# Eight groups of a conditioning product, moved from TensorE to POOL

## The reference, cut to what matters

```python
mod = silu(c) @ w_ada + b_ada          # w_ada 1024 x 6144: six vectors of 1024
h   = rmsnorm(x) * (1 + scale) + shift # the first two, for the token mixer
...                                    # mixer: window attention, gated scan, grouped attention
x   = x + gate_1 * mixer(h)            # the third
h2  = rmsnorm(x) * (1 + scale_2) + shift_2   # the fourth and fifth
x   = x + gate_2 * moe(h2)             # the sixth
```

## Time and profile before

| | |
|---|---|
| median of 3 executions | 820.46 us |
| span of the profiled execution | 816.3 us |
| PE busy | 758.7 us, 93% |
| POOL busy | 25.0 us, 3% |
| DVE busy / ACT busy | 274.9 us / 104.2 us |
| mean granted TensorE clock | 0.990 |

### The profile page before, as it was taken

One profiled execution on the slowest core, in us unless ns is written; L12 is line 12 of the kernel. 1 busy time (PEld: TensorE's weight loads), 2 busy tenths in 40 slices (PEclk: granted clock), 3 DMA queues, 4 the chain that ended last, 5 costly groups with the idle time before them and its releaser, 6 DMA issues.

```text
span 816.3 us, 8564 instructions
## 1 busy us (share of the span) xinstructions
PE 758.7 (93%) x3562; PEld 437.1 (54%) x3562; DVE 274.9 (34%) x484; ACT 104.2 (13%) x185; POOL 25.0 (3%) x44
## 2 busy tenths in 40 slices
PE   5889989999999999999999999995999999999994
PEld 2344676666774377666676587443443443443431
DVE  1422325544200647433332323246203212212323
ACT  4010110000001322212212500020000000000011
POOL 0100000000000006000000000000000000000000
PEclk9999999999999999999999999998999999999998
DMA  9842243020210322754336727951899999987951
GB/s 376 335 200 104 103 136 148 0 104 1 104 52 1 119 100 102 298 206 175 141 136 271 307 106 325 395 190 42 348 373 419 429 419 420 430 338 295 427 216 54
DMA packets 13571, 178.46 MB, mean 219 GB/s; under 512 B 1504, under 2 KB 1632, under 8 KB 2528
## 3 DMA queue, kind: packets, MB, share of 16 engines
q1 hardware_dynamic: 13104, 176.56, 54.0%
q10 hardware_dynamic: 432, 1.40, 0.4%
HBM read 176.91 MB, written 1.05 MB: 218 GB/s over the span
## 4 chain that ended last, share of the span: by engine, by line
PE 86%; DVE 6%; DMA 3%; issue 3%; DVEq 1%; ACT 1%; SPq 0%; POOL 0%; PEldq 0%; ACTq 0%
PE bank L971 20%; PE bank L657 15%; PE bank L651 10%; PE bank L661 8%; PE bank L674 5%; PE bank L959 4%; PE bank L703 4%; PE bank L680 3%; DMA sb<-front_w 3%; PE bank L1015 2%; PE bank L645 2%; PE bank L802 2%; PE bank L823 2%; PE bank L667 2%; PE bank L810 1%
## 5 line engine op out<-in xcount | busy, mean ns | idle before, releaser
L971 PE MATMUL bank<-sb 128*64 128x512 f32 x768 | 166.8, 593 | 3.4 <-DVE sb L1427 2.8
L657 PE MATMUL bank<-sb 128*128 128x256 f32 x576 | 128.2, 381 | 2.4 <-PE bank L645 1.3
L657 PEld LDWEIGHTS bank<-sb 128*128 128x128 f32 x576 | 108.1, 190 | 23.2 <-issue 9.1
L971 PEld LDWEIGHTS bank<-sb 128*64 128x64 f32 x768 | 54.4, 137 | 113.7 <-issue 109.8
L651 PE MATMUL bank<-sb 128*128 128x512 f32 x192 | 85.4, 602 | 3.9 <-DVE sb L1106 3.6
L661 PE MATMUL bank<-sb 128*128 128x512 f32 x160 | 70.0, 593 | 0.3 <-PE bank L657 0.3
L1153 DVE COPY sb<-bank 128x512 f32<-128x512 f32 x45 | 29.4, 686 | 117.7 <-PE bank L810 83.2
L651 PEld LDWEIGHTS bank<-sb 128*128 128x128 f32 x192 | 36.6, 194 | 48.6 <-issue 45.4
L661 PEld LDWEIGHTS bank<-sb 128*128 128x128 f32 x160 | 29.9, 190 | 36.4 <-issue 36.4
L674 PE MATMUL bank<-sb 128*128 128x256 f32 x192 | 42.2, 380 | 0.6 <-PE bank L674 0.6
L1437 DVE TENSOR_TENSOR sb<-sb,bank 128x512 f32<-128x512 f32 x8 | 5.5, 688 | 101.7 <-PE bank L971 89.3
(11 more groups left out here) (210 smaller groups left out, 581.4 us busy)
## 6 DMA issues: line engine op xcount, KB each, us to landing
sb<-expert_w SPq DMA_DIRECT2D x48, 2048.0 KB, 12.2
sb<-front_w SPq DMA_DIRECT2D x32, 2048.0 KB, 8.1
sb<-xcT SPq DMA_DIRECT2D x2, 1024.0 KB, 7.5
sb<-na_bias SPq DMA_DIRECT2D x1, 1536.0 KB, 10.9
sb<-front_w SPq DMA_DIRECT2D x1, 1024.0 KB, 5.0
sb<-b_rows SPq DMA_DIRECT2D x1, 1024.0 KB, 10.3
sb<-x_nat SPq DMA_DIRECT2D x1, 1024.0 KB, 12.3
out<-sb SPq DMA_DIRECT2D x4, 256.0 KB, 2.6
```

The costliest lines, as they stand in the source:

```text
L657: ins = pe.matmul(ps[:, c * L:(c + 1) * L], lhs(w, k, (2 * i + c) * P), hT[:, k, 0:L], start=(k == 0), stop=(k == KD - 1))
L971: ins = pe.matmul(bank[e * CAP:(e + 1) * CAP, :], lhsT[:, k, e * CAP:(e + 1) * CAP], slot[s + e][:, k * cols[0] + cols[1]:k * cols[0] + co ...
```

## The change: groups 4 to 11 made on POOL

TensorE no longer multiplies the slots of ada4 to ada11. POOL, after its work on the grouped attention's q and k, multiplies the whole slot (128x4096) by silu(c), one value per partition and block of 512, in place; three adds fold 4096 columns to 2048, 1024 and 512, the last one into `ada_place(g)`. A semaphore `w_summed` then releases the slot and the turn. `ada_turn` sums over the partitions: one matmul with `ones` for the row groups, the same four transposes for the others, of which DVE now reduces all 128 columns. The group's turn stands one step behind the last fill of the next gate: before steps 8, 10, 12 and 14 for groups 4 to 7, behind step 15 for groups 8 to 11. From the third group on, POOL waits ahead of its multiply until the turn of the group two before it is done (they share a place). The fillers are one per step.

```diff
+POOLED = [f"ada{g}" for g in range(4, 12)]
+GROUPS = ["ada0", "ada2", "ada1", "ada3", "ff"] + [n for n in FRONT[5:] if n not in POOLED]
...
+for _i, _n in enumerate(FILLER):
+    FILLER_AT[_i * STEPS // len(FILLER)].append(_n)
+ADA_TURNS = {i: [] for i in range(STEPS + 1)}
+for _g in range(4, 12):
+    _next = [n for n in FRONT[FRONT.index(f"ada{_g}"):] if n[:4] == "gate"]
+    _at = [i for i in range(STEPS) if _next and fill_no(_next[0], 1) in FILLER_AT[i]] + [STEPS]
+    ADA_TURNS[min(_at[0] + 1, STEPS)].append(_g)
...
+        def wait_free(eng, n):
+            eng.wait_ge(w_summed if FRONT[n] in POOLED else w_used, taken(n))
...
+            pool.wait_ge(c_ready, 1)
+            for i, name in enumerate(POOLED):
+                n, g = FRONT.index(name), int(name[3:])
+                pool.wait_ge(w_in_[SLOT_OF[n]], 16 * (len(earlier(n)) + 1))
+                if i > 1:
+                    pool.wait_ge(shared_ready, shared_no("ada", g - 2) + 1)
+                w = slot[SLOT_OF[n]]
+                wk = w.rearrange("p (k c) -> p k c", k=KD)
+                link(pool.tensor_tensor(wk, wk, cvec[:, :, 0:1].broadcast_to([P, KD, 512]), ALU.mult))
+                link(pool.tensor_tensor(w[:, 0:2048], w[:, 0:2048], w[:, 2048:4096], ALU.add))
+                link(pool.tensor_tensor(w[:, 0:1024], w[:, 0:1024], w[:, 1024:2048], ALU.add))
+                link(pool.tensor_tensor(ada_place(g), w[:, 0:512], w[:, 512:1024], ALU.add))
+                pool.sem_inc(w_summed, 1)
...
             def ada_turn(g):
-                wait_emptied(pe, fill_no(f"ada{g}"))
+                if g < 4:
+                    wait_emptied(pe, fill_no(f"ada{g}"))
+                else:
+                    pe.wait_ge(w_summed, g - 3)
                 ps = take_shared(shared_no("ada", g))
                 src = ada_place(g)
                 if g in ROW_GROUPS:
-                    ins = pe.matmul(ps[:, :], sm("stream0"), src, start=True, stop=True)
+                    ins = pe.matmul(ps[:, :], ones, src, start=True, stop=True)
```

More of the change, by code:

```diff
@@ L51 @@
 USES = [SLOT_OF.count(s) for s in range(FSLOTS)]
-GROUPS = ["ada0", "ada2", "ada1", "ada3", "ff"] + FRONT[5:]
+POOLED = [f"ada{g}" for g in range(4, 12)]
+GROUPS = ["ada0", "ada2", "ada1", "ada3", "ff"] + [n for n in FRONT[5:] if n not in POOLED]
 def taken(n):
-    return GROUPS.index(FRONT[n]) + 1
+    return (POOLED if FRONT[n] in POOLED else GROUPS).index(FRONT[n]) + 1
 def earlier(n):
@@ L100 @@
 FILLER = [n for n in range(fill_no("gq"), fill_no("br0"))]
-def cost(n):
-    return 1 if FILLS[n][0][:3] == "ada" else 4
 FILLER_AT = {i: [] for i in range(STEPS)}
[L108 to L111, removed]
+for _i, _n in enumerate(FILLER):
[5 more added lines that the diff above has]
+    ADA_TURNS[min(_at[0] + 1, STEPS)].append(_g)
 G_STEP = [i for i in range(STEPS) if fill_no("gkv", 1) in FILLER_AT[i]][0]
@@ L122, in ada_in_step @@
 def ada_in_step(i):
-    return [int(FILLS[n][0][3:]) for n in FILLER_AT.get(i, []) if FILLS[n][0][:3] == "ada"]
+    return ADA_TURNS.get(i + 1, [])
 for _i in range(STEPS + 1):
@@ L271, in build @@
         w_in_ = [sem(f"weights_in{i}") for i in range(SLOTS)]
-        w_used = sem("weights_used")
+        w_used, w_summed = sem("weights_used"), sem("weights_summed")
         fill_ready = sem("fill_ready")
@@ L326, in _ @@
                 if earlier(n):
-                    sp.wait_ge(w_used, taken(earlier(n)[-1]))
+                    wait_free(sp, earlier(n)[-1])
                 cols = SLOT // 2 if name == "gkv" else SLOT
@@ L384, in _ @@
                 if s < FSLOTS:
-                    sp.wait_ge(w_used, taken([n for n in range(len(FRONT)) if SLOT_OF[n] == s][-1]))
+                    wait_free(sp, [n for n in range(len(FRONT)) if SLOT_OF[n] == s][-1])
                 load(s, (s % 2) * 3 + s // 2)
@@ L520, in fill @@
                         act.wait_ge(shared_ready, shared_no("ada", g - 1) + 1)
-                    elif g > 5:
-                        act.wait_ge(shared_ready, shared_no("ada", g - 2) + 1)
                     act.activation(ada_place(g), ps[:, :], ACT.Copy).then_inc(done, 1)
@@ L1085, in add_ada @@
                 else:
-                    parts = ps[:, :].rearrange("p (c q s) -> p c s q", c=4, q=4)[:, :, 0:2, :]
-                    dve.tensor_reduce(mod[:, 4 * g:4 * g + 4, :], parts, AX.X, ALU.add).then_inc(shared_out, 1)
+                    if g < 4:
+                        parts = ps[:, :].rearrange("p (c q s) -> p c s q", c=4, q=4)[:, :, 0:2, :]
+                        dst = mod[:, 4 * g:4 * g + 4, :]
+                    else:
+                        parts, dst = ps[:, :].rearrange("p (c q) -> p c q", c=4), mod[:, 4 * g:4 * g + 4, 0]
+                    dve.tensor_reduce(dst, parts, AX.X, ALU.add).then_inc(shared_out, 1)
             b_ada = sm("b_ada")
@@ L1506 @@
 SMALL = 0
-for _name, *_dims in (("ident", P), ("ones", P), ("below", P), ("stream0", P), ("iota", CAP), ("eps", 1), ("limits", MAXPASS - 1),
+for _name, *_dims in (("ident", P), ("ones", P), ("below", P), ("iota", CAP), ("eps", 1), ("limits", MAXPASS - 1),
                       ("rank", NE), ("b_ada", 48), ("g_mix", KD), ("g_ffn", KD), ("lb", 8), ("hg_g", 1),
@@ L1534, in shape_constants @@
         "below": (i[:, None] < i[None, :]).astype(f),
-        "stream0": np.tile((i[:, None] % 32 == 0).astype(f), (1, P)),
         "iota": np.tile(np.arange(CAP, dtype=f), (P, 1)),
```

## The result

The changed kernel takes 857.25 us (median of 4, 855.77 to 858.67) where the kernel before takes 820.14 (median of 4): ratio 1.0458, 95% interval 1.043 to 1.0485, 37 us slower. The forecast was 847.5 us, 27 slower. Its profiled span is 856.8 us, its mean granted clock 0.959 instead of 0.990, POOL is busy 146.9 us instead of 25.0.

A forecast was written before the change was run, and what follows sets the result against it. TensorE was taken as the bound, with 86% of the chain; fills and turns save 19.9 us, but POOL waits, gate5's load and the clock make the first branch 27.0 late: span 843.3 plus 4.2 gives 847.5 us, range 838 to 859.

The forecast's parts named there:

- the hold: Half of DVE's normalising pair stands still for a whole POOL instruction and ends 0.28 us after it.
- the walk: Step-by-step timing of the new kernel through the attention steps: first branch fill at 491.3 instead of 464.34, span 843.3 us.
- (b): Rival, chance 0.13: POOL is slower on long rows, T = 18 us a group with a multiply of 9.1; 857.6 us.
- (d): Rival, chance 0.10: stalls inside steps each cost half clock, 3 times 1.6 us, and one more hold of 4; 856 us.
- What POOL needs for a group: POOL's multiply 7.1 us and adds 4.7, 2.4 and 1.3, from slopes of shorter rows: T = 15.9 us a group.
- (c): Rival, chance 0.04: not slower, POOL at the one-input cast's pace, T = 7.5 us, pair stalls nearly vanish; 820.6 us.
- The wait at the end: Behind step 15, POOL's groups 10 and 11 take 31.8 us; turns to first branch fill 36.3 us instead of 4.5.
- the clock's 1.6: TensorE restarts at the half clock level after the long idle behind group 11: 1.6 us lost, added once.
- Waits inside the steps: DVE's normalising pairs, held beside POOL's long instructions, make steps 6, 7 and 8 late by 2.9, 5.3 and 2.1 us.
- rival (a): Chance 0.16: POOL holds DVE only briefly, stalls of steps 6 to 8 go, b_rows costs 4.5 us at step 8; 842.0 us.
- gate5's load: Load into gate4's slot, no longer covered by two ada fills: it lands at 435.7, its fill 3.4 us late.
- Nothing behind it changes: Behind the first branch fill no further cost: the expert loads keep their distance to TensorE.

## Why the prediction was right, and where it was short

The direction, the hold and the long waits came out as forecast; 847.5 was 10 us short of 857.25, and closer than the working deserves. By the walk itself the first branch fill was 11.5 us short (491.3 for 502.78) and the span 13.5 (843.3 for 856.8): 2.1 more were lost behind the branches, 4.2 us around the span instead of 1.8 gave 2.4 back, and the median lies 1.3 below the profiled execution. The number was inside the range only because this reached up to (b) and (d), and (b) did not happen, and (d) only by half. By its own steps:

- *What POOL needs for a group.* 15.5 us measured, 15.9 forecast: multiply 7.03 (7.1), adds 4.53, 2.40 and 1.28 (4.7, 2.4, 1.3). Slopes from rows of 128 to 1024 columns held up to 4096. Rivals (b) and (c) fall with it; that (b)'s 857.6 is nearly the measured time is chance.
- *The wait at the end.* From step 15's turned probabilities (465.72) to the first branch fill 37.1 us, forecast 37.9 with the clock. Four places took one of the two waits away, idle matmuls the clock's 1.6 (1.6 forecast).
- *Waits inside the steps.* Idle 1.98, 3.33 and 2.11 us in steps 6 to 8, forecast 2.9, 5.3 and 2.1. The hold itself is as forecast, the second half of a pair waits for the next instruction as well: 7.21 us for 343.64 to 350.85, the end of the first add (350.57) plus 0.28, as in the earlier trace rows. Pieces of 512 columns cut it to the length of a piece: rival (a) is out as to its mechanism. Its b_rows wait is real, though, and appears as soon as the holds go. Step 7's wait is shorter than forecast because TensorE, at the half clock behind step 6's wait, came to it later; POOL set its end. The 1.3 us of half clock behind step 7's wait (transposes in 1.11 us for 0.66, group 4's turn in 1.92 for 1.10) were not in the sum: the forecast took none for the shorter stalls and kept 3 us for them in the range. From step 4's scores to step 15's turned probabilities it measured 147.8 us, the walk 144.8; these 1.3 and gate5's 1.7 are the difference.
- *gate5's load.* 3.85 us, forecast 3.4, and 1.7 of half clock in the fill behind it (8.83 for 7.14), also not in the sum.
- *Rival (d)'s half clock.* Its first half came true: three stalls, in steps 0, 7 and 14, cost a spell at the half level each, 1.5, 1.3 and 1.7 us, where it had 3 times 1.6. Its second half, one more hold of 4 us, did not: the three holds cost 7.4 us of idle, less than the 10.3 of the walk. So its 856 is near for a reason that it did not have, step 0.
- **The missing term is step 0.** The walk said "gq's two fills are now in two steps, so step 4 begins 3.3 us after 305.33", as if nothing but TensorE's own work stood in step 0. But DVE has the scan's readout ahead of step 0's maxima, 10 us from the reciprocals on; two gq fills of 14 us covered it, one of 7.1 does not. Step 0 took 15.24 us instead of about 9, and the run with short reciprocals got 5.5 us of it back. With the half clock in step 1's scores (1.74 for 1.13) step 0 is the largest part of the 11.5 us. I followed every fill that was removed and not the one that was moved; its cover was the rest of step 0.
- The other 2.6 us (step 0's scores at 270.90 instead of 268.34) arose ahead of all that changed: the same instructions ran in both, with three spells at the half clock in this execution and one in that of before. It is an execution's own and no part of the change: in the ten profiles of the experiments, whose work up to there is the same, step 0's scores begin anywhere from 267.94 to 271.09. So are the 2.1 us behind the branches, where the same experts' matmuls at the half clock took 6.13 and 15.31 us for 5.34 and 13.95. "Nothing behind it changes" holds for the work; the clock differed.

## What to carry to other kernels

An engine that is idle most of the time is not free: before you move work there, look in the trace for who stands still beside it and how long one instruction holds it, and cut the instructions so that a hold is shorter than the slack of whoever waits. Look at the last pieces of the moved work, since their wait for a buffer decides whether they lie beside work or behind all of it. And when a plan of fillers changes, ask of each filler what it was covering: here two ada fills covered a load and a gq fill covered a chain on DVE.

## What the runs showed that I had not expected

- A multiply on POOL with one value spread along the row goes at 1.7 ns a column (7033 ns for 4096), an add of two tiles at 2.2 (4533 for 2048): on the same engine the add takes 29% more a column.
- In the changed kernel TensorE's waits of 5.15, 3.33 and 3.85 us in steps 0, 7 and 14 were each followed by work at the half granted clock, worth 1.3 to 1.7 us (2.7 behind 3.29 us in the run with only the last add), so such a wait cost some 30 to 80% more. With shorter waits it varied: behind 1.98 us in step 6 the clock fell (0.56 from 352 to 354 us), behind the same 1.98 us in the run with four places it did not (1.00), nor behind 2.11 us in step 8; and with 3.66 us at gate5 in the run with idle matmuls the fill took 7.15 us, at full clock.
- DVE's products of two SBUF tiles are held too (0.69 us alone, 1.75 beside POOL), not only the tensor_scalars, and POOL in turn is held: seven adds of 512 columns took 8.81 us alone and 10.03 beside those products and a normalising pair.
